# From the last FFN step to the mixer's first weights: residual inside the FFN's accumulation, LayerNorm scale and shift applied as columns, beta and decay from unsplit tokens

## The chip, the core and the metric

The program runs on one NeuronCore of a Trainium2 chip. The metric is the device time of one execution in microseconds (us), taken as the median of several runs. The core has TensorE (PE, matrix products, with its weight loads shown as PEld), VectorE (DVE), ScalarE (ACT), GpSimd (POOL) and SyncE (SP), which issues the large weight loads. Each engine works through its own instructions in order, and they wait for each other by semaphores.

## What is computed

Two transformer blocks on 256 tokens of width 1024. The first block is attention, then a convolutional feed-forward net (FFN) with residual, then an RMS norm. The second block puts 16 meta tokens in front, applies a LayerNorm, and runs a hybrid mixer (a gated delta rule and a stick-breaking attention), and a mixture of 32 experts. Only the passage between the two blocks is touched:

```python
x = x + _conv_ffn(_rmsnorm(x, norm_ffn[i]), ffn_w_up[i], ffn_conv_w[i], ffn_conv_b[i], ffn_w_down[i])
return _rmsnorm(x, norm_final)
...
h = layer_norm(jnp.concatenate([meta, x], axis=1), ln_emb_g, ln_emb_b)   # ((x - mu) * rsqrt(var + 1e-5)) * g + b
...
proj = x @ w_in
dn_qkv, dn_z, dn_b, dn_a, sb_qkv, gates = jnp.split(proj, SPLIT_POINTS, axis=-1)
beta = jax.nn.sigmoid(dn_b)
g = -jnp.exp(dn_a_log) * jax.nn.softplus(dn_a + dn_dt_bias)
```

The LayerNorm follows an RMS norm, so both are done at once: with y = x * norm_final, the layer norm of y divided by x's root mean square is (y - mean(y)) / sqrt(var(y) + eps), where eps is 1e-5 times (mean(x*x) + 1e-6).

## The kernel before

**Tiles.** X holds the 256 tokens as two tiles t = 0, 1 of 128 tokens by 1024 features. For products the tokens are turned: hT_hi and hT_lo hold 8 blocks k of 128 features by 272 tokens (16 meta, 256 others). A float32 product is made of three float32r products, hi*hi, hi*lo and lo*hi (`split3`, lines 1933 to 1935), so each operand is split: ACT copies to float32r (hi), DVE subtracts (lo).

**Weights** come in granules of 2048 columns. SP loads a granule into one of three buffers `raw` (line 610; the load of granule n waits until granule n - 3 has been split), ACT makes `whi` (`hi_part`, line 827), DVE makes `wlo` (`lo_part`, line 1298). whi and wlo have two buffers each, and a few granules have their own (`OWN_SLOT`). Granules 16 to 48 are the FFN's, granule 49 (`G_IN`) and 50 are the mixer's z gate, 51 and on its q, k and v. Granule 49 shares its buffer with granule 47.

**Last FFN step.** PE adds granule 48's products (`down`) into four banks PM, 12 matmuls a token tile, 24 in all. At the start of the FFN four bf16 matmuls of a zero row clear the banks (line 2093). A semaphore after token tile 0 (`s_ffn`) and one at the end (`s_gran`) let DVE go on.

**Seam** (lines 1451 to 1489 on DVE, 958 to 979 on ACT, 2131 to 2152 on PE). For each token tile DVE adds the banks to X, multiplies by norm_final with a running sum; ACT squares X and the centred product, with sums; ACT takes the root, DVE multiplies by the LayerNorm's scale row and, in two halves, by the reciprocal root and adds the shift row. PE turns each half (4 transposes of 128 by 128). ACT and DVE split them. In between PE does 16 small products for the router's constants (36 columns each) and dummy products of 128 by 128 (`keep_warm`, line 1993).

**Beta and decay.** Eight columns of w_in (`wba`) are split too, and `ba` is 24 matmuls (8 blocks, three products). The result is turned by `baT`, and DVE and ACT make beta and the decay from it in steps on 12 columns (`decays`, lines 1582 to 1584, and `softplus`, lines 1588 to 1601).

**Order.** After the seam a list `plan` sets the order for all engines. It begins: ba; granule 49's first half; baT; decays; its second half; softplus; granule 50; masks; granule 51. On DVE, `lo_part` of granule 51 stands at "granule 50", so behind softplus.

Of the kernel before, what the change touches and what calls it, by code (L numbers as in the profile page):

```python
# [87 lines left out]
def build(nc, a, out):  # L88
    with ExitStack() as ctx:
# [14 lines left out]
        def con(name, n=None, rows=P):  # L104
# [15 lines left out]
        OWN_SLOT = (14, 15, 48)  # L120
# [9 lines left out]
        scratch = place("scratch", [P, TT, D], PH + 49152)  # L130
        scratch2 = place("scratch2", [P, TT, D], PH + 57344)
# [3 lines left out]
               for n, at in zip(OWN_SLOT, (PH + 74752, PH + 24576, PH + 24576))}  # L135
# [6 lines left out]
        zero = place("zero", [1, D], PH + 96256, BF16)  # L142
# [15 lines left out]
        zsum, nmu, vs, ve = tiny(TT), tiny(TT), tiny(TT), tiny(TT)  # L158
        mx, nmx, psum_, rinv = tiny(8), tiny(8), tiny(8), tiny(8)
# [16 lines left out]
        s_zero, s_x2 = sem("s_zero"), sem("s_x2")  # L176
# [10 lines left out]
        assert OWN_SLOT == (G_WO + 2, G_WO + 3, G_IN - 1)  # L187
# [302 lines left out]
        E_STEPS = {"baT": 1, "norm": 2, "D": 1, "orms": 1, "Zs": 3}  # L490
# [47 lines left out]
        wr_experts = place("wr_experts", [P, GROUPS, KD, EPG], PH + 65536)[:, :, :, :]  # L538
        wr_groups = place("wr_groups", [P, KD, GROUPS], PH + 65536 + 4 * NE * KD)[:, :, :]
# [154 lines left out]
        def _(pool):  # L694
# [19 lines left out]
            pool.dma_start(vrow[112:113, 1, :], a["dn_norm_g_2"]).then_inc(s_vrow, 16)  # L714

            pool.wait_ge(s_cols, 1)
# [26 lines left out]
            pool.memset(ba, 0.0).then_inc(s_init, 1)  # L743
            pool.memset(sbk[:, :, NT:3 * P], 0.0).then_inc(s_init, 1)
# [73 lines left out]
        def _(act):  # L818
# [91 lines left out]
            act.wait_ge(s_colsT, 1)  # L910
            act.activation(cols[:, 0:P + 113], PM[:, 1, 0:P + 113], ACT.Copy).then_inc(s_cols, 1)
# [12 lines left out]
            act.wait_ge(s_cols, 1)  # L924
# [10 lines left out]
            def ffn_step(n, j, par, it, first=False, last=False):  # L935
# [8 lines left out]
                if not last:  # L944
                    hi_part(n + 3, it)
                act.wait_ge(s_hid, j + 1)
                act.activation(hid_hi[:, par, :, :], hid[:, par, :, :], ACT.Copy).then_inc(s_hidhi, 1)
                if not first:
                    hi_part(n + 4, it)
# [8 lines left out]
            act.wait_ge(s_wba, 48)  # L958
# [328 lines left out]
        def _(dve):  # L1287
# [165 lines left out]
            for t in range(TT):  # L1453

                if t == 0:
                    dve.wait_ge(s_ffn, 1)
                else:
                    dve.wait_ge(s_gran, G_IN)
# [1188 lines left out]
```

## Time and profile before

| | us |
|---|---|
| median of 3 runs | 858.91 |
| lowest, highest | 858.44, 859.41 |
| the profiled execution | 859.89 |
| its span, first to last instruction | 857.8 |

The span is the part that the trace shows; some 2 us of the execution lie around it. The profile has a page with the busy time of each engine, a chain of the work that ended last, and views of stretches: instructions in order of time, and busy time with the granted clock. PE's matmuls are pipelined: a row's duration reaches from its start to a modelled end, and the distance between starts is what a matmul costs in a row of them. A plain float32 matmul shows as two records.

### The profile page before, as it was taken

The page shows a single profiled execution, that of the slowest core. Times are in us where ns is not written, and L with a number is a line of the kernel's source. Part 1 is how long each engine was busy: PE and PEld are TensorE (multiplying, and loading weights), DVE is VectorE, ACT ScalarE, POOL GpSimd, SP SyncE. Part 2 cuts the span into 40 slices and gives each one's busy share as a digit, 9 for nine tenths or more (in the row PEclk, how much of TensorE's full clock was granted, in tenths as well). Part 3 has the DMA queues.
Part 4 walks back from the last instruction along what each step waited for, and adds up shares of the span by engine and source line. Part 5 has one row for each costly group of instructions (what it writes and reads, how often), then busy time and mean ns, then how long its engine had stood idle before and what let it go on. Part 6 is the DMA issues. An engine that isn't in the chain of part 4 may idle for free.

```text
span 857.8 us, 16132 instructions
## 1 busy us (share of the span) xinstructions
PE 831.0 (97%) x6642; PEld 681.0 (79%) x6642; DVE 483.9 (56%) x829; ACT 374.0 (44%) x559; POOL 57.7 (7%) x91
## 2 busy tenths in 40 slices
PE   6999999999999999999999999999999999999994
PEld 6999999999999988998898999999755555555541
DVE  4455667776667777666733445486753333333335
ACT  4555764455545554566453454654321111111113
POOL 0200041000000000100110000000110000000010
PEclk9999999999999998999999999999999999999998
DMA  9864362555555561444333232559889999999981
GB/s 289 272 218 136 128 194 83 182 192 193 173 180 187 196 196 56 142 129 146 119 99 99 90 110 66 181 196 412 341 335 408 409 409 409 408 409 409 409 352 50
DMA packets 102129, 193.29 MB, mean 225 GB/s; under 512 B 4589, under 2 KB 70464, under 8 KB 101936
## 3 DMA queue, kind: packets, MB, share of 16 engines
q1 hardware_dynamic: 99664, 185.61, 60.3%
q0 software_dynamic: 1824, 4.60, 1.7%
q10 hardware_dynamic: 576, 2.14, 0.7%
q8 instruction: 49, 0.80, 0.4%
q14 instruction: 16, 0.13, 0.0%
HBM read 191.29 MB, written 1.05 MB: 224 GB/s over the span
## 4 chain that ended last, share of the span: by engine, by line
PE 87%; DVE 6%; ACT 3%; issue 2%; DMA 1%; ACTq 0%; DVEq 0%
PE PG L1933 14%; PE PG L2503 13%; PE PG L1935 13%; PE PG L1934 13%; PE PG L2525 7%; PE PM L2534 4%; PE PM L1933 2%; PE PM L1935 2%; PE PM L1934 2%; ACT whi L827 2%; PE PG L2512 1%; PE PM L2357 1%; DVE wlo L1298 1%; PE PG L1993 1%; PE PM L2475 1%
## 5 line engine op out<-in xcount | busy, mean ns | idle before, releaser
L1933 PE MATMUL PG<-hT_hi,whi 128*128 128x256 f32 (+1 forms) x832 | 240.1, 289 | 0.0
L1935 PE MATMUL PG<-hT_hi,wlo 128*128 128x256 f32 (+1 forms) x832 | 235.0, 282 | 0.0
L1934 PE MATMUL PG<-hT_lo,whi 128*128 128x256 f32 (+1 forms) x832 | 234.9, 282 | 0.0
L1298 DVE TENSOR_TENSOR wlo<-raw,whi 128x2048 fp32r<-128x2048 f32 x75 | 171.8, 2290 | 76.5 <-ACT whi L827 76.3
L1933 PEld LDWEIGHTS PG<-hT_hi,whi 128*128 128x128 f32 x832 | 156.9, 189 | 5.9 <-issue 2.6
L1935 PEld LDWEIGHTS PG<-hT_hi,wlo 128*128 128x128 f32 x832 | 157.1, 189 | 0.0
L1934 PEld LDWEIGHTS PG<-hT_lo,whi 128*128 128x128 f32 x832 | 156.5, 188 | 0.2
L827 ACT ACTIVATE whi<-raw 128x2048 fp32r<-128x2048 f32 x75 | 143.2, 1910 | 25.5 <-PE PG L1935 22.6
L2503 PE MATMUL PG<-expert_w,xw 128*64 128x256 f32 x992 | 113.9, 382 | 0.0
L1860 DVE SCALAR_TENSOR_TENSOR y_lo<-PG,small,y_hi 128x512 fp32r<-128x512 f32 x32 | 24.0, 750 | 133.2 <-ACT y_hi L1229 133.2
L2503 PEld LDWEIGHTS PG<-expert_w,xw 128*64 128x64 f32 x992 | 68.6, 137 | 37.0 <-issue 5.8
L2525 PE MATMUL PG<-expert_w,hid 128*64 128x512 f32 x256 | 61.9, 604 | 0.0
L1229 ACT ACTIVATE y_hi<-PG,small 128x512 fp32r<-128x512 f32 x32 | 22.0, 688 | 85.6 <-PE PG L2525 85.6
L1223 ACT ACTIVATE gusum<-PG 128x256 f32<-128x256 f32 x32 | 12.3, 385 | 97.2 <-PE PG L2503 97.2
L2525 PEld LDWEIGHTS PG<-expert_w,hid 128*64 128x64 f32 x256 | 15.6, 136 | 29.7 <-issue 29.6
L1933 PE MATMUL PG<-whi,hT_hi 128*128 128x256 f32 x128 | 36.8, 288 | 1.3 <-DVE hT_lo L1560 0.9
L1935 PE MATMUL PG<-whi,hT_lo 128*128 128x256 f32 x128 | 36.0, 281 | 0.0
L1934 PE MATMUL PG<-wlo,hT_hi 128*128 128x256 f32 x128 | 35.9, 281 | 0.0
L786 POOL COPY xw<-pair 128x512 f32 x31 | 19.6, 634 | 200.5 <-PE PG L2503 182.2
L1933 PE MATMUL PM<-whi,hid_hi 128*128 128x512 f32 x80 | 31.6, 395 | 0.2 <-DVE wlo L1298 0.2
L1935 PE MATMUL PM<-whi,hid_lo 128*128 128x512 f32 x80 | 31.2, 390 | 0.0
L1934 PE MATMUL PM<-wlo,hid_hi 128*128 128x512 f32 x80 | 31.2, 390 | 0.0
(496 smaller groups left out, 1289.8 us busy)
## 6 DMA issues: line engine op xcount, KB each, us to landing
expert_w<-in_expert_w_gate SPq DMA_DIRECT2D x64, 512.0 KB, 15.4
expert_w<-in_expert_w_up SPq DMA_DIRECT2D x64, 512.0 KB, 15.8
expert_w<-in_expert_w_down SPq DMA_DIRECT2D x32, 1024.0 KB, 17.0
raw<-in_ffn_w_up SPq DMA_DIRECT2D x22, 1024.0 KB, 5.1
raw<-in_w_in SPq DMA_DIRECT2D x22, 1024.0 KB, 5.2
raw<-in_moba_w_qkv SPq DMA_DIRECT2D x12, 1024.0 KB, 6.0
raw<-in_ffn_w_down SPq DMA_DIRECT2D x11, 1024.0 KB, 4.8
raw<-in_moba_w_o SPq DMA_DIRECT2D x4, 1024.0 KB, 5.1
```

The source lines that it names most:

```text
L786: pool.tensor_copy(xw[i2][:, :, :], pair[:, :, bass.ds(at, WIN)]).then_inc(s_win, 1)
L827: act.activation(hi_of(n), raw[:, n % R, :], ACT.Copy).then_inc(s_hi, 1)
L1223: act.activation(gusum[i2][:, :], PG[:, i2, 0:EFF], ACT.Copy).then_inc(s_gu, 1)
L1229: act.activation(y_hi[:, :], result, ACT.Copy, scale=slotw[i2]).then_inc(s_yhi, 1)
L1298: dve.tensor_tensor(lo_of(n), raw[:, n % R, :], hi_of(n).bitcast(F32), ALU.subtract).then_inc(s_lo, 1)
L1860: dve.scalar_tensor_tensor(y_lo[:, :], result, slotw[i2], y_hi[:, :].bitcast(F32), ALU.mult, ALU.subtract).then_inc(s_y, 1)
L1933: pe.matmul(dst, lh, rh, start=start, stop=False, **kw)
L1934: pe.matmul(dst, lh, rl, start=False, stop=False, **kw)
L1935: return pe.matmul(dst, ll, rh, start=False, stop=stop, **kw)
L2503: mm = pe.matmul(PG[WIN * h:WIN * h + WIN, i2, 0:EFF], x[:, KH * kind + k, :], w[:, h, k, :], start=kind + k == 0, stop=kind == 1 and k == ...
L2525: mm = pe.matmul(result[WIN * h:WIN * h + WIN, :], hid2[i2][:, f, :], w[:, f, 512 * h:512 * h + 512], start=f == 0, stop=f == 1)
L2534: mm = pe.matmul(PM[:, 2 * t + h, :], hot[i2][x, P * t:P * t + P], y[x, :], start=first and y is y_hi, stop=last and y is y_lo)
```

## The change

1. The zero matmuls go. The four banks are begun with X itself, by float32 matmuls of the identity (`start_sums`, 128 by 512). Three stand where 10 of 12 dummy products were, the last where the zero matmuls were. After the FFN the banks hold X plus its sum.
2. Granule 49 gets an own buffer. On ACT its hi part moves ahead of `hid_hi`.
3. DVE multiplies the banks by norm_final straight away. Token tile 0's mean and variance come from bn_stats and bn_aggr, tile 1's from a running sum on DVE and a square on ACT. X gets only (y - mean) / root, by `tensor_scalar` halves.
4. PE turns these. Scale and shift are applied on the turned tokens, per 128-feature block, into `h_cols`: blocks 0 to 3 by DVE, 4 to 7 by ACT, four instructions a token tile each. Two more rows of DMA and one more small transpose bring them as columns (`ln_cols`). The split reads h_cols.
5. `ba` is 8 plain float32 matmuls of h_cols, in two halves of the array (output rows 0 to 7 and 64 to 71), and `baT` 6 small matmuls that add the halves.
6. The rows of X still need scale and shift for the mixer's residual: `shifted_rows`, 8 `tensor_tensor` of 512 columns, each waiting for the one before, between `lo_part` of granule 50 and the plan.
7. Router products and dummy products on PE are put in another order. Three memsets on POOL wait for granule 49.

```diff
+            start_sums(0, 0)
+            start_sums(0, 1)
+            start_sums(1, 0)
+            keep_warm(2, con("ident"), con("ident"), PM[:, 3, :])
             norm_T(1, 1)
             pe.wait_ge(s_ev, evacs(G_FFN - 1))
-            for b in range(4):
-                pe.matmul(PM[:, b, :], zero[0:1, 0:P], zero[0:1, 0:512], start=True, stop=True)
+            start_sums(1, 1)
...
+            def columns(t):
+                act.wait_ge(s_xT, 11 + 2 * t)
+                for k in range(KH, KD):
+                    act.activation(h_cols[:, k, META + P * t:META + P * t + P], PM[:, 2 * t + 1, P * (k - KH):P * (k - KH) + P], ACT.Identity,
+                                   scale=ln_cols[:, 0, k:k + 1], bias=ln_cols[:, 1, k:k + 1]).then_inc(s_hcolsa, 1)
...
+            def columns_hi(t, f):
+                act.wait_ge(*((s_hcolsv, KH * t + KH) if f == 0 else (s_hcolsa, 1 + KH * t + KH)))
+                c = slice(META + P * t, META + P * t + P)
+                ln_hi(hT_hi[:, 4 * f:4 * f + 4, c], h_cols[:, 4 * f:4 * f + 4, c])
...
+            def shifted_rows(t):
+
+                for f in range(2):
+                    c = slice(D // 2 * f, D // 2 * f + D // 2)
+                    step(dve.tensor_tensor(X[:, t, c], X[:, t, c], rows[:, 3, c], ALU.mult))
+                    step(dve.tensor_tensor(X[:, t, c], X[:, t, c], rows[:, 0, c], ALU.add))
...
             lo_part(G_IN + 1)
+            shifted_rows(0)
+            shifted_rows(1)
             for st in plan:
...
+                    for k in range(0, KD, 2):
+                        if k == KH:
+                            pe.wait_ge(s_hcolsa, 1 + KD)
+                        for h in range(2):
+                            mm = pe.matmul(bank[WIN * h:WIN * h + 8, 0:NT], wba[:, k + h, :], h_cols[:, k + h, :], start=k == 0, stop=k == KD - 2)
```

**DVE, from the seam's last splits to the decays.** The hT_lo rows are the last splits of the turned tokens, wlo is granule 50, the rows on `small` are `decays`. Before:

```order
L1481 TENSOR_TENSOR hT_lo<-PM,hT_hi 128x4x128 [waits s_xhi] x4
L1298 TENSOR_TENSOR wlo<-raw,whi 128x2048 [waits s_hi]
L1582 TENSOR_TENSOR small<-small 128x12 [waits s_wba,pm_free1]
L1583 TENSOR_SCALAR small<-small 128x12 [waits s_dve]
L1584 TENSOR_TENSOR small<-small 128x12 [waits s_dve]
```

Now:

```order
L1527 TENSOR_TENSOR hT_lo<-h_cols,hT_hi 128x4x128 [waits s_xhi] x4
L1326 TENSOR_TENSOR wlo<-raw,whi 128x2048 [waits s_hi]
L1534 TENSOR_TENSOR X<-X,rows 128x512
L1535 TENSOR_TENSOR X<-X,rows 128x512 [waits s_dve]
L1534 TENSOR_TENSOR X<-X,rows 128x512 [waits s_dve]
...
L1630 TENSOR_TENSOR small<-small 128x12 [waits s_wba,pm_free1,s_dve]
```

Eight row operations now stand between granule 50's split and the decays.

**PE, from the router's products to `ba`.** `PG<-small` and `PG<-bwr` are the router's products, `PG<-cst` 128x128 dummy products, `PM<-cst,X` the transposes. Before:

```order
L2138 MATMUL PG<-small,cst 128x36 x7
L2140 MATMUL PG<-bwr,cst 128x36 x8
L2142 MATMUL PG<-small,cst 128x36 [waits s_wr]
L1993 MATMUL PG<-cst 128x128 x2
L2148 MATMUL PM<-cst,X 128x128 [waits s_h]
L2148 MATMUL PM<-cst,X 128x128 x3
...
L1993 MATMUL PG<-cst 128x128 x6
```

Now, from tile 0's second half (the rows left out are three more such groups, and the first transposes of tile 1 end the piece):

```order
L2202 MATMUL PM<-cst,X 128x128 [waits s_h]
L2202 MATMUL PM<-cst,X 128x128 x3
L2195 MATMUL PG<-small,cst 128x36
L2196 MATMUL PG<-bwr,cst 128x36
L2041 MATMUL PG<-cst 128x128
...
L2210 MATMUL PG<-small,cst 128x36 [waits s_wr]
L2041 MATMUL PG<-cst 128x128 x3
L2202 MATMUL PM<-cst,X 128x128 [waits s_h]
L2202 MATMUL PM<-cst,X 128x128 x3
```

Half of the router's products moved behind token tile 0's transposes, each pair with a dummy product, and they stand ahead of tile 1's.

**ACT, from tile 1's turned tokens to granule 50.** `mean_wr` is a copy of the router's sums. Before:

```order
L973 ACTIVATE hT_hi<-PM 128x4x128 [waits s_xT] x4
L982 ACTIVATE mean_wr<-PG 128x36 [waits s_logit]
L982 ACTIVATE mean_wr<-PG 128x36
L827 ACTIVATE whi<-raw 128x2048 [waits s_gran,landed2]
L1002 ACTIVATE baT<-PM 8x272 [waits pm_full0]
```

Now:

```order
L999 ACTIVATE h_cols<-PM,small 128x128 [waits s_xT]
L999 ACTIVATE h_cols<-PM,small 128x128 x3
L983 ACTIVATE hT_hi<-h_cols 128x4x128 [waits s_hcolsv]
L983 ACTIVATE hT_hi<-h_cols 128x4x128 [waits s_hcolsa]
L1015 ACTIVATE mean_wr<-PG 128x36 [waits s_logit]
L1015 ACTIVATE mean_wr<-PG 128x36
L830 ACTIVATE whi<-raw 128x2048 [waits s_gran,landed2]
```

Four column operations came in ahead of tile 1's two copies, and so ahead of granule 50's hi part.

## Rows read from the trace of the kernel before

**Rows 1.** The page: busy us of each engine (share of the span), instructions.

```profile
PE 831.0 (97%) x6642; PEld 681.0 (79%) x6642; DVE 483.9 (56%) x829; ACT 374.0 (44%) x559; POOL 57.7 (7%) x91
```

**Rows 2.** Chain that ended last, over the seam: start, us, what.

```profile
318.06 1.93 ACT whi L827
320.01 1.36 DVE wlo L1298
...
336.19 1.79 PE PG L1993 x16
```

**Rows 3.** PE in order of time: start, us, engine, line, what.

```profile
323.95 0.67 PE L2133 MATMUL PG<-cst,MT 16*128 16x16 f32 x8
324.55 1.98 PE L2138 MATMUL PG<-small,cst 128*128 128x36 f32 x16
...
328.25 0.41 PE L2142 MATMUL PG<-small,cst 1*128 1x36 f32 x2
...
330.18 1.97 PE L2148 MATMUL PM<-cst,X 128*128 128x128 f32 x8 [0.72 <-DVE X L1476]
...
340.80 0.28 PE L1933 MATMUL PG<-hT_hi,whi 128*128 128x256 f32 x1
```

**Rows 4.** PE where granule 51 begins.

```profile
352.59 0.35 PE L1933 MATMUL PG<-hT_hi,whi 128*128 128x272 f32 x1
```

**Rows 5.** DVE in order of time, 316 to 355 us.

```profile
316.11 0.69 DVE L1430 TENSOR_TENSOR hid<-cgate,cup 128x512 f32<-128x512 f32 x1
...
323.61 1.23 DVE L1463 CUSTOM_DVE_ANT_0 XN<-X,rows 128x1024 f32<-128x1024 f32 x1
...
344.58 0.17 DVE L1582 TENSOR_TENSOR small<-small 128x12 f32<-128x12 f32 x1 [3.44 <-ACT small L1002]
...
346.30 0.17 DVE L1588 TENSOR_SCALAR small<-small 128x12 f32<-128x12 f32 x1 [1.14 <-ACT small L1090]
...
350.14 2.29 DVE L1298 TENSOR_TENSOR wlo<-raw,whi 128x2048 fp32r<-128x2048 f32 x1
352.35 0.68 DVE L1606 TENSOR_TENSOR dN<-cst,small 128x512 f32<-128x512 f32 x1
```

**Rows 6.** ACT in order of time, 312 to 346 us.

```profile
312.52 1.02 ACT L932 ACTIVATE cup<-PG,cols 128x256 f32<-128x256 f32 x2 [0.53 <-PE PG L1935]
316.84 0.63 ACT L947 ACTIVATE hid_hi<-hid 128x512 fp32r<-128x512 f32 x1 [3.29 <-DVE hid L1430]
...
336.72 0.29 ACT L982 ACTIVATE mean_wr<-PG 128x36 f32<-128x36 f32 x2
336.88 1.93 ACT L827 ACTIVATE whi<-raw 128x2048 fp32r<-128x2048 f32 x1
...
345.86 0.21 ACT L1088 ACTIVATE small<-small 128x12 f32<-128x12 f32 x1
```

**Rows 7.** Stretches: us, PE, PEld, DVE, ACT, POOL busy, PEclk, DMA, GB/s.

```profile
328.00:330.00 2.00, 1.46 (x9) 1.08 (x8) 1.65 (x3) 1.07 (x3) 0.00 (x0) 0.75 0.00 0
330.00:332.00 2.00, 1.82 (x9) 1.82 (x10) 2.00 (x4) 0.98 (x3) 0.00 (x0) 0.50 0.00 0
...
334.00:336.00 2.00, 2.00 (x12) 2.00 (x11) 1.09 (x2) 0.40 (x1) 0.00 (x0) 0.55 0.03 8
...
403.00:405.00 2.00, 0.59 (x5) 0.42 (x4) 1.99 (x3) 0.38 (x1) 0.00 (x0) 1.00 0.00 0
```

**Rows 8.** PE elsewhere: the FFN's start, and two forms in the expert stage.

```profile
128.38 1.03 PE L1927 MATMUL PG<-cst,XN 128*128 128x128 f32 x8
...
133.87 1.32 PE L1927 MATMUL PG<-cst,XN 128*128 128x128 f32 x8 [0.34 <-DVE XN L1384]
135.13 1.03 PE L2093 MATMUL PM<-zero 1*128 1x512 bf16 x4
...
824.87 3.67 PE L2503 MATMUL PG<-expert_w,xw 128*64 128x256 f32 x32
...
831.74 1.02 PE L2545 MATMUL PM<-X,alpha_ident 128*128 128x512 f32 x2
```

More of the change, by code:

```diff
@@ L129, in build @@
         oT_lo = place("oT_lo", [P, KD, SEQ], PH + 57344, F32R)
-        scratch = place("scratch", [P, TT, D], PH + 49152)
-        scratch2 = place("scratch2", [P, TT, D], PH + 57344)
+        squares_of = [place(f"squares{i}", [P, D], PH + 71680 + 4096 * i) for i in range(3)]
         prob = place("prob", [P, 2, 2, 3 * P], PH + 98304)
@@ L923, in _ @@
             norm_hi(1, [1])
-            act.wait_ge(s_cols, 1)
+            act.wait_ge(s_cols, 2)
             def col(i, n=1):
@@ L945, in ffn_step @@
                     hi_part(n + 3, it)
+                else:
+                    hi_part(n + 4, it)
                 act.wait_ge(s_hid, j + 1)
                 act.activation(hid_hi[:, par, :, :], hid[:, par, :, :], ACT.Copy).then_inc(s_hidhi, 1)
-                if not first:
+                if not first and not last:
                     hi_part(n + 4, it)
@@ new lines, in _, with ln_hi @@
+            squares(0)
+            act.wait_ge(s_ve, 1)
+            act.activation(lnrt[:, 0:1], lnmv[:, 1:2], ACT.Sqrt, bias=ve[:, 0:1]).then_inc(s_lnrt, 1)
+            def ln_hi(dst, src):
+                act.activation(dst, src, ACT.Copy).then_inc(s_xhi, 1)
+            act.wait_ge(s_xT, 9)
+            act.activation(h_cols[:, :, 0:META], PG[:, 0, 0:P].rearrange("p (k n) -> p k n", k=KD), ACT.Copy).then_inc(s_hcolsa, 1)
+            act.wait_ge(s_hcolsa, 1)
+            ln_hi(hT_hi[:, :, 0:META], h_cols[:, :, 0:META])
@@ L1465, in _, with two @@
-            for t in range(TT):
+            dve.wait_ge(s_rows, 64)
+            dve.wait_ge(s_ffn, 1)
+            def two(x):
+                return x.rearrange("p (h n) -> p h n", h=2)
+            dve.tensor_tensor(two(XN[:, 0, :]), PM[:, 0:2, :], two(rows[:, 2, :]), ALU.mult).then_inc(s_x2, 1)
+            dve.wait_ge(s_x2, 1)
+            for b in range(2):
+                step(dve.bn_stats(lnst[:, 6 * b:6 * b + 6], XN[:, 0, D // 2 * b:D // 2 * b + D // 2]))
+            step(dve.bn_aggr(lnmv[:, 0:2], lnst[:, 0:12]))
@@ L2262, in _ @@
                     for c, (t0, n) in enumerate(CH):
-                        mm = pe.transpose(bank[0:n, 8 * c:8 * c + 8], baT[:, t0:t0 + n], con("ident", 8, 8))
+                        for h in range(2):
+                            mm = pe.matmul(bank[0:n, 8 * c:8 * c + 8], baT[:, h, t0:t0 + n], con("ident", 8, 8), start=h == 0, stop=h == 1)
                     mm.then_inc(full(*st), 1)
```

188 lines of the change are left out of this document (100 added, 88 removed).

## The prediction

> **What bounds the kernel now.** The page comes first: PE is busy 97% of the span, DVE 56%, ACT 44% [rows 1]. So time is won or lost where PE waits or does filler. The chain of waits gives such a place. For 18 us, from 318.06 to 336, it runs through ACT's and DVE's split of granule 49 and DVE's and ACT's norm, and it ends in PE's transposes and dummy products [rows 2]. PE in order of time tells the same: it leaves the FFN at 323.95, does router products and fillers, waits 0.72 us for DVE's first half, and takes up weights of the mixer, granule 49, at 340.80 [rows 3]. That is 16.9 us in which it does little that counts.
>
> The second place to read is the one behind it, where a gain must pass. Granule 51 begins on PE at 352.59 [rows 4]. On DVE its split runs from 350.14, and the next instruction starts at 352.35 [rows 5]. So PE is served 0.2 us ahead of need. Ahead of that split DVE does the decays and softplus, and before the decays it idles 3.44 us [rows 5].
>
> Last the clock. The granted clock falls from 2.4 to 1.2 GHz at 329.0 (0.75 on average over 328 to 330), after the stretch of 36-column products, and is back at 2.4 GHz only at about 335.8 (0.55 over 334 to 336); an idle time of 1.4 us near 404 left it at 2.4 GHz [rows 7].
>
> **FFN start: +0.1 us.** Three 512-column sums replace ten dummies. One such matmul in the expert stage shows as 1.02 us with its end [rows 8], 0.87 from start to start, so three and two dummies of 0.22 are 3.05 us from 130.8. PE is then at 133.85, where it anyway waits until 133.87 for DVE [rows 8]. The fourth costs 0.9 to 1.0 against 0.96 for the zero matmuls it replaces (135.13 to 136.09) [rows 8]. The extra small transpose on PE lies on the path, 0.1 us. Its two DMAs, one ACT copy, and POOL's later queue (0.25 us) are hidden: ACT and POOL idle there for longer.
>
> **Seam on DVE and ACT.** Granule 49's hi part now runs on ACT from 313.5 to 315.5, in the 3.29 us in which ACT waits for `hid` [rows 6]; nothing but hid_hi is queued behind it. DVE splits it right behind hid_lo, 318.2 to 320.4, and starts the norm when PE has ended token tile 0, the twelfth of the 24 matmuls that end at 323.95, at 321.4 instead of 322.4. DVE then does a product (1.25 us by the row of 1024 columns [rows 5]), two statistics of 512 columns (0.65 each, an estimate from the 0.69 of a 512-column operation [rows 5]), three small ones and tile 1's product, 1.25. Its first half of X is there at 326.5, the second at 327.0. PE comes for it at 323.95 + 0.6 for the meta transposes + 2.7 for half the router products = 327.3 and does not wait. Of those products 16 take 324.55 to 328.25, 0.23 each [rows 3], and each pair has a dummy of 0.22. So the wait of 0.72 us is gone, and PE sets the pace next.
>
> **Seam on PE.** From 327.3: two half tiles of four transposes at 0.11 each, 0.9 (eight took 1.03 with the end at 2.4 GHz [rows 8]), 328.2; the other router products 2.7, 330.9; the bias product 0.3 and three dummies 0.7, 331.9; tile 1's transposes 0.9, 332.8. DVE's halves of tile 1 would be there at 330.5, since ACT's two squares and root end by 329.2. Eight dummies bring PE to 334.5. Then `ba`. Sixteen float32 matmuls of 256 columns in two halves of the array took 3.67 us [rows 8], so eight of 272 columns are 1.95 us: 336.45. If the halves did not run side by side it would be 3.9. It needs h_cols at 334.3 (below) and granule 49 needs the last split at 336.2; both are met. **PE takes up granule 49 at 336.45 instead of 340.80, 4.35 us sooner** [rows 3].
>
> **Where that goes.** PE then does 11.8 us of work until granule 51 (340.80 to 352.59 in rows 3 and 4), plus 0.3 for the three more baT matmuls, and arrives at 348.55. What it waits for there:
> - tile 1's turned tokens, 332.85;
> - ACT's four column operations. No row has 128 columns with scale and bias; two of 256 take 1.02 us [rows 6], 0.46 from start to start, and 128 columns fewer save 0.1: 0.36 each, 1.45 together, 334.3. The ends are 0.2 (a plain small copy) and 0.46, so 0.8 to 1.9;
> - two hT_hi copies of 512 columns at 0.55, 335.4; mean_wr 0.16 (336.72 to 336.88), granule 50's hi part 1.93 [rows 6], 337.5;
> - DVE's split of it, 2.25 as for granule 51 [rows 5], 339.75;
> - the eight row operations. Each is like the 512-column product of 0.69 [rows 5] plus 0.03 for its wait: 5.75, 345.5. What hid nothing before is now in front of the decays: these stand behind it in DVE's queue, and ACT's exponentials and softplus behind them;
> - three decays 0.6, 346.1. Before, ACT's next step waited for a table load until 345.86 [rows 6]; now the table is long there;
> - ACT 0.44 (345.86 to 346.30), softplus 3.84 (346.30 to 350.14), the split 2.25 [rows 5, 6]: 352.65.
>
> **So granule 51 starts at 352.7, where it started at 352.59.** The gain of 4.35 us ends in a wait of PE of 4.15 us, and 0.1 is lost. Bounds: the column operations 0.8 to 1.9, the row operations 0.66 to 0.75 each; together -1.0 to +0.8.
>
> Here a page gives another price. The Trainium skill, "VectorE: DVE Perf Modes", section on the TRN2 errata, has 172 + columns cycles at 1.2 GHz for a ScalarE operation from PSUM, 0.25 us for 128 columns; by it the columns take 1.0, not 1.45, and the sum comes 0.45 lower. The same section warns of many small tiles for this fixed part, which speaks against eight column operations where there was none. The 256-column row shows more than that formula, so I keep to the row.
>
> **The clock behind the wait: +1.7 us.** The trace has no idle time of PE of 4 us in its middle. One of 1.4 us left the clock up [rows 7]; a stretch of thin work of some 5 us took it down. 4.15 us with nothing is more than either, so I take it that the clock falls. In the one case shown it stayed at 1.2 GHz for 5.5 us after PE took up work again (330.18 to 335.8) [rows 3, 7]; all work behind 352.7 is dense, so each microsecond there at 1.2 GHz costs half. That is 0 to 2.75; I take 1.7, above the middle, because the row's 5.5 held idle time and thin work and this stretch does not last so long, but a fall is likelier than none. The Trainium skill, "TensorE: Matmul & The Clock Gate", Part 1, says that the slow state is the default and activity lifts it; by that the fall is certain, and the sum would hold.
>
> Does anything take this up later? The split of granule 52 and the masks on DVE follow that of 51 directly and end at 358.0, before PE wants granule 52 even by the old time of 360.9. Behind that the kernel is PE's, and the experts' loads wait for PE's progress. So it passes through. POOL's three memsets now run at 342.5, 18 us before POOL's next task.
>
> **Sum:** 0.1 + 0.1 + 1.7 = +1.9 us. The profiled execution took 859.89 with a span of 857.8; that is 1 us above the median of 858.91. On the median: **860.8 us**.
>
> **Rivals.**
> *The clock also falls in the seam.* It did before, and the router products are as thin as before. Against it: the dummies between them, and no idle time. If it falls at 329, the work of PE from there (2.0 router, 0.3, 0.7, 0.9) takes up to 3.6 us more, and all that hangs on 332.85 moves by as much: +3.6 + 1.9 = 864.4. Decides: the clock over 329 to 333. 0.23.
> *The wait without the cost.* PE waits some 4 us, the clock stays up, and 858.3 to 859.9 comes out, nearest 859.1. It needs a clock that rides over an idle time three times that of the row. 0.17.
> *The row operations are cheap* (the rival on the other side). If an operation of 512 columns in SBUF cost 0.42 instead of 0.72, eight would give back 2.4 us, PE would wait 1.8, too short for the clock to fall: granule 51 at 350.3, 856.7. It decides from about 0.5 each. The 0.69 row speaks against it. With it I count anything unseen that shortens DVE's chain. 0.10.
> *My forecast*, 859.6 to 861.9: 0.50.
>
> **Numbers.** 0.2%, 1.7 us, is about what a measurement can tell from no change: 857.2 to 860.6. Of the forecast's 0.50 some 0.18 falls under 860.6; of the first rival all is slower; the second is no change. Slower 0.55, same 0.35, faster 0.10. The range has to take in most of the clock rival and the lower end of the cheap wait: 858.2 to 864.0.
>
> **What the new profile would show.** PE takes up granule 49 near 336.5 and waits about 4 us before granule 51 for the split on DVE; the eight row operations stand from 339.8 to 345.5 with 0.69 each; the granted clock is 1.00 from 324 to 350 and lower behind 351. I am wrong if PE's first matmul of granule 51 comes without a wait, if the clock falls before 333, or if `ba` takes near 4 us.

## The result, and the profile after

The changed kernel takes 860.93 us (median of 7 runs, 860.43 to 862.50), where the kernel before took 858.85 beside it (857.92 to 859.41). The ratio is 1.0029, with a 95% interval of 1.0020 to 1.0039: slower by 2 us. The profiled execution took 860.89 with a span of 859.0, against 859.89 and 857.8 before. Two kernels below have one slow execution each, of 1027 and of 4567 us: the ratios leave these out, the medians 857.66 and 862.24 don't, and without them they would be 857.54 and 861.75. Lines of `kernel.py` below are those of the changed kernel unless a section says otherwise.

The page first, which answers to [rows 1]:

```profile
PE 829.3 (97%) x6634; PEld 677.8 (79%) x6634; DVE 487.1 (57%) x840; ACT 375.4 (44%) x567; POOL 58.2 (7%) x93
```

PE is busy 1.7 us less than before and the span is 1.2 us longer. So PE waits more, 2.9 us in all. The view of PE in order of time shows where (start, us, engine, line, what, and in brackets the idle time before it and what ended it):

```profile
323.99 0.67 PE L2188 MATMUL PG<-cst,MT 16*128 16x16 f32 x8
...
327.38 1.04 PE L2202 MATMUL PM<-cst,X 128*128 128x128 f32 x8
...
332.13 1.04 PE L2202 MATMUL PM<-cst,X 128*128 128x128 f32 x8
333.00 1.95 PE L2041 MATMUL PG<-cst 128*128 128x128 f32 x16
334.88 2.01 PE L2324 MATMUL PM<-h_cols,small 128*8 128x272 f32 x16
336.82 0.38 PE L1981 MATMUL PG<-hT_hi,own_hi 128*128 128x256 f32 x1
...
339.85 1.24 PE L2332 MATMUL PM<-cst,baT 8*128 8x8 f32 x12
```

```profile
353.20 0.56 PE L1981 MATMUL PG<-hT_hi,whi 128*128 128x272 f32 x1 [3.43 <-DVE wlo L1326]
```

Granule 49 is taken up at 336.82, where it was 340.80 [rows 3]: 4.0 us won. Granule 51 begins at 353.20, where it was 352.59 [rows 4]: the 4.0 us are gone, and 0.6 more, in a wait of 3.43 us for DVE's split. DVE in order of time shows what stands ahead of that split, and answers to [rows 5]:

```profile
321.45 1.23 DVE L1484 TENSOR_TENSOR XN<-PM,rows 128x1024 f32<-128x1024 f32 x1 [0.98 <-PE PM L1983]
...
337.76 2.29 DVE L1326 TENSOR_TENSOR wlo<-raw,whi 128x2048 fp32r<-128x2048 f32 x1 [1.21 <-ACT whi L830]
339.97 0.68 DVE L1534 TENSOR_TENSOR X<-X,rows 128x512 f32<-128x512 f32 x1
340.69 0.69 DVE L1535 TENSOR_TENSOR X<-X,rows 128x512 f32<-128x512 f32 x1
...
345.77 0.17 DVE L1630 TENSOR_TENSOR small<-small 128x12 f32<-128x12 f32 x1
...
346.92 0.17 DVE L1636 TENSOR_SCALAR small<-small 128x12 f32<-128x12 f32 x1 [0.56 <-ACT small L1118]
...
350.76 2.29 DVE L1326 TENSOR_TENSOR wlo<-raw,whi 128x2048 fp32r<-128x2048 f32 x1
352.97 0.68 DVE L1654 TENSOR_TENSOR dN<-cst,small 128x512 f32<-128x512 f32 x1
```

From 339.97 to 345.77 DVE does the eight row operations (two of them are shown). Before, the decays began at 344.58, after an idle time of 3.44 us [rows 5]; now they begin at 345.77 behind work. ACT in order of time answers to [rows 6]:

```profile
313.51 1.92 ACT L830 ACTIVATE own_hi<-raw 128x2048 fp32r<-128x2048 f32 x1
...
333.21 1.50 ACT L999 ACTIVATE h_cols<-PM,small 128x128 f32<-128x128 f32 x4 [0.88 <-PE PM L2202]
334.59 1.16 ACT L983 ACTIVATE hT_hi<-h_cols 128x512 fp32r<-128x512 f32 x2
...
346.48 0.21 ACT L1116 ACTIVATE small<-small 128x12 f32<-128x12 f32 x1 [3.61 <-DVE small L1632]
```

Last the clock. Stretches with busy time by engine and, behind POOL, PE's granted clock, as in [rows 7]:

```profile
328.00:330.00 2.00, 2.00 (x21) 2.00 (x19) 1.43 (x5) 0.39 (x2) 0.00 (x0) 1.00 0.00 0
...
350.00:352.00 2.00, 0.00 (x0) 0.00 (x0) 1.86 (x5) 2.00 (x2) 0.00 (x0) 1.00 0.00 0
352.00:354.00 2.00, 0.80 (x3) 0.83 (x4) 2.00 (x3) 0.26 (x1) 0.00 (x0) 0.70 0.00 0
354.00:356.00 2.00, 2.00 (x10) 2.00 (x10) 2.00 (x5) 0.00 (x0) 0.00 (x0) 0.50 0.91 252
356.00:358.00 2.00, 2.00 (x17) 2.00 (x16) 2.00 (x2) 0.00 (x0) 0.00 (x0) 0.95 0.78 272
```

The seam is now at 2.4 GHz throughout. Behind the wait the clock is 1.2 GHz until about 356.2. PE has dense work from 353.20, so some 3 us of it ran at 1.2 GHz, with 10 matmuls in 2 us where 18 are usual. What that cost shows at the first product of a later stage, now and in the profile before:

```profile
360.67 1.95 PE L2349 MATMUL PM<-cst,dN 128*128 128x128 f32 x16
```

```profile
358.71 1.95 PE L2280 MATMUL PM<-cst,dN 128*128 128x128 f32 x16
```

From granule 51's start it is 7.47 us away, and was 6.12: 1.35 us lost. With the 0.61 by which granule 51 starts later that makes 1.96. The span grew by 1.2 only: the profile before has one more fall of the clock, near 610 us (mean 0.86 over 608 to 620, where this profile has 1.00), and its way from 566.74 to its end is 0.8 us longer than the same way here. That place is far behind the change, and five of the twelve profiles in this document have such a fall, whatever the kernel.

### The profile page after: what moved, and what is told of

Its sections match the earlier page's. It is cut to its first block, busy times and chain, and to the rows that moved or that the text cites. A ratio compares the mean times of both kernels' runs of the same rounds, so it can differ in the third digit from the quotient of the medians.

```text
span 859.0 us, 16131 instructions
## 1 busy us (share of the span) xinstructions
PE 829.3 (97%) x6634; PEld 677.8 (79%) x6634; DVE 487.1 (57%) x840; ACT 375.4 (44%) x567; POOL 58.2 (7%) x93
## 4 chain that ended last, share of the span: by engine, by line
PE 85%; DVE 8%; ACT 4%; issue 2%; DMA 1%; ACTq 0%; DVEq 0%
PE PG L1981 13%; PE PG L2572 13%; PE PG L1983 12%; PE PG L1982 12%; PE PG L2594 7%; PE PM L2603 4%; PE PM L1981 2%; PE PM L1982 2%; PE PM L1983 2%; ACT whi L830 2%; DVE wlo L1326 2%; PE PG L2581 1%; PE PM L2426 1%; PE PG L2041 1%; PE PM L2057 1%
## 5 line engine op out<-in xcount | busy, mean ns | idle before, releaser
L1981 PE MATMUL PG<-hT_hi,whi 128*128 128x256 f32 (+1 forms) x816 | 236.2, 289 | 3.4 <-DVE wlo L1326 3.4
L1983 PE MATMUL PG<-hT_hi,wlo 128*128 128x256 f32 (+1 forms) x816 | 231.1, 283 | 0.0
L1982 PE MATMUL PG<-hT_lo,whi 128*128 128x256 f32 (+1 forms) x816 | 231.0, 283 | 0.0
L1326 DVE TENSOR_TENSOR wlo<-raw,whi 128x2048 fp32r<-128x2048 f32 x74 | 169.5, 2291 | 74.6 <-ACT whi L830 74.5
L1981 PEld LDWEIGHTS PG<-hT_hi,whi 128*128 128x128 f32 x816 | 154.6, 189 | 9.7 <-issue 6.5
L1983 PEld LDWEIGHTS PG<-hT_hi,wlo 128*128 128x128 f32 x816 | 154.7, 190 | 0.0
L1982 PEld LDWEIGHTS PG<-hT_lo,whi 128*128 128x128 f32 x816 | 154.2, 189 | 0.2
L830 ACT ACTIVATE whi<-raw 128x2048 fp32r<-128x2048 f32 x74 | 141.3, 1909 | 24.9 <-PE PG L1983 22.5
```

The costliest lines, as they stand in the source:

```text
L830: act.activation(hi_of(n), raw[:, n % R, :], ACT.Copy).then_inc(s_hi, 1)
L1326: dve.tensor_tensor(lo_of(n), raw[:, n % R, :], hi_of(n).bitcast(F32), ALU.subtract).then_inc(s_lo, 1)
L1981: pe.matmul(dst, lh, rh, start=start, stop=False, **kw)
L1982: pe.matmul(dst, lh, rl, start=False, stop=False, **kw)
L1983: return pe.matmul(dst, ll, rh, start=False, stop=stop, **kw)
```

## The experiments

The theory: DVE's chain (tile 1's turned tokens, columns, copies, split, eight row operations, decays, softplus, split) sets the start of granule 51, so what PE wins at granule 49 becomes a wait, and the wait takes the clock down. The rivals: another link sets granule 51; the clock's fall costs nothing; the fall comes from the seam. Where a ratio is given, it is against runs of the kernel before on the same chip. The profiles differ by up to 0.5 us already where PE leaves the FFN, and no view shows why; a table behind the last run counts from there.

### The row operations later

```diff
             lo_part(G_IN + 1)
-            shifted_rows(0)
-            shifted_rows(1)
...
                         lo_part(n + 1)
+                    if n in (G_IN + 2, G_IN + 3):
+                        shifted_rows(n - G_IN - 2)
```

> The changed kernel with one edit: the eight row operations on X stand on VectorE behind the splits of granules 52 and 53 (four behind each), no longer ahead of the decays. My theory, that the gain at granule 49 is lost again in VectorE's chain ahead of granule 51 and that the clock falls in PE's wait there: the chain ends 5.8 us sooner than it must, so PE takes up granule 51 without a wait at about 349.8 (changed kernel: 353.20 after 3.43 of waiting), the granted clock is 1.00 over 350 to 356, and the time is 3.4 + 1.45 = 4.9 us below the changed kernel: 856.0, 0.997 of the kernel before. Rival A, the wait is real but the clock's fall costs nothing: 857.5. Rival B, what holds granule 51 is not the row operations but another link (exponentials, table load, the raw buffer of granule 51): granule 51 stays near 353 and the time at 860.9. Rival C, the row operations only move the wait to granules 52 to 54, where VectorE has splits and masks to do: 351 is early but a wait of 2 us or more shows behind it, and the time is 858 to 860.

Measured: 856.31 us, ratio 0.9967 (0.9955 to 0.9980). PE at granule 51, then a stretch:

```profile
349.69 0.36 PE L1981 MATMUL PG<-hT_hi,whi 128*128 128x272 f32 x1
```

```profile
352.00:354.00 2.00, 2.00 (x18) 2.00 (x17) 2.00 (x3) 0.08 (x1) 0.00 (x0) 1.00 0.97 345
```

No wait, 3.5 us sooner (0.2 of it by an earlier end of the FFN), and the clock stays up. The row operations were the link. They don't pass the wait on to granules 52 to 54: from granule 51 to the later stage PE takes 6.12 us, as in the kernel before. Rivals A, B and C fall: 4.6 us of the 4.9 expected are there by the medians, 5.3 by the ratios.

### Filler inside the wait

```diff
                         pe.wait_ge(s_ev, evacs(n - 2))
+                        if n == G_IN + 2:
+                            keep_warm(14, con("ident"), con("ident"))
```

> The changed kernel with one edit: PE does 14 dummy products of 128 by 128 (about 3.0 us of dense work at 2.4 GHz) just ahead of granule 51, inside the wait for its split. Nothing else moves, and VectorE's chain ends at the same time, so granule 51 still begins at 353.2 to 353.3. Theory (the fall of the clock in the wait costs 1.45 us): the granted clock is 1.00 over 352 to 358, and the time is 1.4 to 1.5 us below the changed kernel, 859.4 to 859.5, 1.0007 of the kernel before. Rival A (the clock's fall costs nothing, or falls anyway): same as the changed kernel, 860.9 (1.0024). Rival D (dummies come out too long and stand in the way of granule 51): 861 or more, with granule 51 later than 353.5.

Measured: 859.06 us, ratio 1.0006 (0.9996 to 1.0016). PE around granule 51, and the stretch behind it:

```profile
349.24 3.29 PE L2041 MATMUL PG<-cst 128*128 128x128 f32 x28
352.75 0.39 PE L1981 MATMUL PG<-hT_hi,whi 128*128 128x272 f32 x1 [0.22 <-DVE wlo L1326]
```

```profile
354.00:356.00 2.00, 2.00 (x19) 2.00 (x18) 2.00 (x5) 0.00 (x0) 0.00 (x0) 1.00 0.98 329
```

Here PE still can't begin before DVE is done, and it does nothing useful in the meantime; the time falls by 1.9 us all the same, and the rival by which the fall of the clock costs nothing is out. Granule 51 stands 0.45 sooner than in the first profile, but 0.37 of that is an earlier end of the FFN. From granule 51 to the later stage PE takes 6.15 us, 1.3 less than the 7.47 of the first profile and 2.7 less than the 8.88 of the repeat below; the 1.9 of the medians lies between. In three of 11 executions the mean granted clock was 0.994 and the time 860.2 to 860.5, in the others 0.995 or 0.996; where it fell in those three no trace shows. A fall near 610 would explain some 0.7 of the 1.1 to 1.4 us that they took more.

### Half the row operations

```diff
             shifted_rows(0)
-            shifted_rows(1)
```

> The changed kernel with one edit: the four row operations of token tile 1 are left out, so that the residual of tile 1 in the mixer lacks LayerNorm's scale and shift; this is a probe of time. It doses the suspected cost. Theory: VectorE's chain is 4 x 0.73 = 2.9 us shorter, granule 51 begins at 350.3 with a wait of about 0.5 us, too short for the clock to fall, and the time is 2.9 + 1.45 = 4.35 us below the changed kernel: 856.6 (0.9974 of the kernel before). Rival A (no cost of the clock): 858.0 (0.999). Rival B (the row operations don't set granule 51): 860.9 (1.0024).

Measured: 857.22 us, ratio 0.9976 (0.9967 to 0.9985). PE at granule 51:

```profile
350.62 0.36 PE L1980 MATMUL PG<-hT_hi,whi 128*128 128x272 f32 x1 [1.03 <-DVE wlo L1326]
```

This kernel leaves the second token tile's residual without scale and shift, so it is a probe of time only. Half the dose moves the start by 2.4 us from the FFN's end (2.6 as the rows stand) where 2.9 was expected, and the clock stayed at 2.4 GHz behind a wait of 1.03 us. The time is 3.7 us below the changed kernel by the medians, where 4.35 was expected. The missing 0.5 at granule 51 stands in one operation of softplus, a `tensor_scalar` of 12 columns, which took 0.68 instead of 0.18. Its cause comes further down.

### Without the dummies between the router's products

```diff
                     pe.matmul(PG[:, 1, 64:64 + NL], con("ones"), bwr[:, k, :], start=False, stop=False, skip_group_check=True)
-                    keep_warm(1, con("ident"), con("ident"))
```

> The changed kernel with one edit: the eight dummy products between the pairs of router products go, so that the 36-column products stand side by side as in the kernel before. It tests the rival of the prediction by which thin products take the clock down in the seam. If they do, the granted clock is below 1.00 somewhere in 328 to 336, tile 1's turned tokens are complete 1 to 2.5 us later than without a fall, and the time is at or above the changed kernel: 861 to 864. If the clock stays up, PE has 8 x 0.22 = 1.8 us less to do, reaches token tile 0 sooner (where it may wait up to 0.5 us for VectorE's first half), turns tile 1 about 1.2 us sooner, VectorE's chain ends about 1.2 us sooner, and the time is 1.2 us below the changed kernel: 859.7 (1.001). I give the fall 0.6, since the kernel before fell behind the same products.

Measured: 859.75 us, ratio 1.0003 (0.9993 to 1.0014), with executions from 857.96 (mean granted clock 0.995) to 861.67 (0.990). The median alone would fit the branch without a fall. The profiled execution, of 861.45 us, shows the other one; stretches, then PE at granule 51:

```profile
326.00:328.00 2.00, 1.97 (x11) 1.94 (x11) 1.45 (x6) 1.44 (x4) 0.00 (x0) 0.55 0.00 0
...
334.00:336.00 2.00, 2.00 (x11) 2.00 (x11) 1.75 (x5) 0.90 (x3) 0.00 (x0) 0.50 0.00 0
```

```profile
355.23 0.36 PE L1981 MATMUL PG<-hT_hi,whi 128*128 128x272 f32 x1 [2.85 <-DVE wlo L1326]
```

The clock was at 1.2 GHz from 326 to 336, and granule 51 came 2.0 us later than in the changed kernel (2.6 from the FFN's end). Yet this wait, of 2.85 us, left the clock up, so the sum is +0.6 against 860.89. The fall in the seam is thus real in this execution. The mean clocks, from 0.990 to 0.995, say that its size differs from one execution to the next, and at 0.995 it may be missing; no trace shows those.

One thing the median does say: this kernel is 1.2 us faster than the changed kernel, by the ratios 2.2, and the intervals of the two ratios don't meet. The eight dummies are 1.8 us of PE's way through the seam, and here they cost more than they saved. One reason is in the profile: with the seam longer, the wait behind it left the clock up. How long the seam was in the faster executions no trace shows; the profiled one is the second longest of ten.

### The kernel before, with dummies between the same products

```diff
                 pe.matmul(PG[:, 1, 0:NL], con("ones"), wr[:, k, :], start=k == 0, stop=k == KD - 1)
+                keep_warm(k % 2, con("ident"), con("ident"))
             for k in range(KD):
                 pe.matmul(PG[:, 1, 64:64 + NL], con("ones"), bwr[:, k, :], start=k == 0, stop=False)
+                keep_warm(k % 2, con("ident"), con("ident"))
...
-            keep_warm(2, con("ident"), con("ident"))
```

> The kernel before with one edit: a dummy product of 128 by 128 behind each second of the 16 router products in the seam, eight more, and the two behind the bias product gone. It asks how much of the changed kernel's gain at granule 49 (4.35 us) was the clock: the kernel before spent 329 to 335.8 at 1.2 GHz. If the dummies keep the clock up, PE comes to tile 0 at 330.4, turns it in 1.0 instead of 2.0 us, does six dummies in 1.3 instead of 2.8, turns tile 1 when VectorE has it (333.0 to 334.1), is through its eight dummies at 335.9 and takes up granule 49 at 338.9 to 339.0 instead of 340.80; VectorE's and ScalarE's steps behind the seam all follow PE's, so granule 51 comes 1.85 us sooner, and the time is 1.85 below the kernel before: 857.1 (0.998). Rival A: the clock falls all the same, at the wait for tile 0's half, and the time is 858.9 to 859.7 (1.000 to 1.001), since eight dummies are added. Rival B: the clock stays up and granule 49 comes sooner, but the decays, which wait for a table load and ba, hold granule 51 at 352.6: 858.9.

Measured: 857.66 us, ratio 0.9985 (0.9976 to 0.9994). PE in order of time (lines of the kernel before), then a stretch:

```profile
330.13 1.09 PE L2149 MATMUL PM<-cst,X 128*128 128x128 f32 x8
...
332.80 1.32 PE L2149 MATMUL PM<-cst,X 128*128 128x128 f32 x8 [0.23 <-DVE X L1476]
...
339.02 0.28 PE L1933 MATMUL PG<-hT_hi,whi 128*128 128x256 f32 x1
...
350.79 0.36 PE L1933 MATMUL PG<-hT_hi,whi 128*128 128x272 f32 x1
```

```profile
330.00:332.00 2.00, 2.00 (x19) 1.95 (x19) 1.93 (x5) 1.34 (x4) 0.00 (x0) 1.00 0.03 8
```

Granule 49 comes at 339.02 instead of 340.80, and granule 51 at 350.79 instead of 352.59. PE left the FFN 0.3 sooner here (323.64 against 323.95), so 1.5 of the 4.0 us that the change won at granule 49 can be had by the dummies alone. In this kernel they pass through, because DVE's decays follow PE and not a queue of their own: 1.5 at granule 51, and 1.3 in the time, where 1.85 was expected.

### The own buffer alone

```diff
-        OWN_SLOT = (14, 15, 48)
+        OWN_SLOT = (14, 15, 48, 49)
...
             pool.memset(ba, 0.0).then_inc(s_init, 1)
+            pool.wait_ge(s_gran, G_IN + 1)
...
+                else:
+                    hi_part(n + 4, it)
                 act.wait_ge(s_hid, j + 1)
...
-                if not first:
+                if not first and not last:
                     hi_part(n + 4, it)
```

> The kernel before with one part of the change alone: granule 49 gets an own buffer, and on ScalarE its hi part stands ahead of hid_hi; scratch tiles move to make room for it. VectorE then splits granule 49 at about 318 and can start the norm when PE ends token tile 0, at 321.4 instead of 322.4. By the prediction's step that is 1.0 us on all that follows, up to granule 51, so long as nothing else holds it: PE comes for tile 0's first half at 329.5, which would then be there, so 0.7 us of PE's wait goes and the rest of the norm comes 1.0 us sooner: 857.9 (0.9988). If the clock then stays up for longer, since the idle time is gone, up to 1.8 us more: 856.1. If the norm is set by ScalarE's squares and not by VectorE's start, nothing is won: 858.9.

Measured: 858.81 us, ratio 1.0001 (0.9992 to 1.0010). The expectation of 1.0 us failed. (The scratch tiles and two router tables are placed elsewhere to make room; the diff leaves that out.) DVE and POOL in order of time, and PE at granule 51 (its own lines):

```profile
320.96 1.22 DVE L1462 TENSOR_TENSOR X<-X,PM 128x1024 f32<-128x1024 f32 x1 [0.79 <-PE PM L1938]
...
344.65 1.37 DVE L1595 TENSOR_SCALAR small<-small 128x12 f32<-128x12 f32 x1
```

```profile
344.59 0.47 POOL L745 MEMSET sbk<- 128x448 f32 x1 [9.24 <-PE PG L1938]
345.00 0.53 POOL L746 MEMSET sbv<- 128x512 f32 x1
345.46 0.53 POOL L747 MEMSET dU<- 128x512 f32 x1
```

```profile
351.24 0.36 PE L1936 MATMUL PG<-hT_hi,whi 128*128 128x272 f32 x1 [1.03 <-DVE wlo L1301]
```

DVE begins the norm sooner, as meant. But an operation on 12 columns, 0.17 elsewhere [rows 5 has others of this size], takes 1.37 and ends at 346.02, as the third memset does (345.46 + 0.53 = 345.99). The memsets have come there because the new buffer shares memory with what the first two of them clear, so they wait for granule 49. PE pays 1.03 us for it. (This profile is of a short execution, 857.81 us, in which the clock fell for less of the seam, 0.86 on average over 324 to 336 against 0.72 before. Granule 51 stands 1.35 us sooner in it than before, 0.4 of it by an earlier end of the FFN, although the median has not moved.)

### The own buffer, with the memsets one granule later

```diff
-            pool.wait_ge(s_gran, G_IN + 1)
+            pool.wait_ge(s_gran, G_IN + 2)
```

> The kernel before with granule 49's own buffer, as in the run with that alone, and GpSimd's three memsets waiting for granule 50 instead of 49. In that run VectorE's tensor_scalar of softplus took 1.37 us beside the memsets (344.65 to 346.02; the third memset ended at 345.99), and PE waited 1.03 us ahead of granule 51, so that the slot's gain of 1.0 us at the norm's start was gone. Theory: the operation takes 0.17, the split ends 1.2 us sooner, the wait goes, and the time is 1.0 us lower: 857.8, 0.9988 to 0.999 of the kernel before. Rival: the gain is covered by where the clock falls in the seam: 858.8, 1.000.

Measured: 857.23 us, ratio 0.9986 (0.9977 to 0.9995). The same operation:

```profile
346.08 0.18 DVE L1595 TENSOR_SCALAR small<-small 128x12 f32<-128x12 f32 x1
```

PE begins granule 51 without a wait. The profiled execution was one with a long fall of the clock in the seam (0.72 over 324 to 336; 858.56 us), so its times are no good for a comparison with the run above; the two ratios are. They differ by 0.0015, 1.3 us, where 1.0 was expected, though the intervals still overlap. The profile before has the same 0.72 in the seam: against it, granule 49 and granule 51 both come 0.6 us sooner, counted from the FFN's end.

### Another order of the seam, and the best version

```diff
             turned_half(0, 1)
-            router_sums(4, KD)
-            pe.wait_ge(s_wr, 176)
-            pe.matmul(PG[:, 1, 64:64 + NL], con("ones", rows=1), rb[0:1, :], start=False, stop=True, skip_group_check=True).then_inc(s_logit, 1)
-            keep_warm(3, con("ident"), con("ident"))
+            router_sums(4, 6)
+            keep_warm(4, con("ident"), con("ident"))
             turned_half(1, 0)
             turned_half(1, 1)
-            keep_warm(8, con("ident"), con("ident"))
+            router_sums(6, KD)
+            pe.wait_ge(s_wr, 176)
+            pe.matmul(PG[:, 1, 64:64 + NL], con("ones", rows=1), rb[0:1, :], start=False, stop=True, skip_group_check=True).then_inc(s_logit, 1)
+            keep_warm(1, con("ident"), con("ident"))
```

> The kernel with the late row operations, and PE's seam in another order: between token tile 0's and tile 1's transposes stand two pairs of router products instead of four, then four dummy products; the last two pairs and the bias product stand behind tile 1's transposes, where eight dummies stood and are gone. PE has as much filler as work there, so the clock should stay at 2.4 GHz. Theory (VectorE's chain from tile 1's turned tokens sets granule 51, with PE close behind): tile 1 is turned at about 331.5 instead of 332.8, the columns, copies and splits behind it come 1.3 us sooner, ba can begin at 333.4 and granule 49 near 335.3, granule 51 near 348.4, and the time is 1.3 us below the late kernel: 855.0, 0.9953 of the kernel before. Rival 1: the clock falls among the router products (four thin pairs behind each other near the end), up to 3 us lost: 856 to 859. Rival 2: VectorE's halves of tile 1 are not there before 331.0, so that only 0.5 us is won: 855.8.

Measured: 855.76 us, ratio 0.9962 (0.9949 to 0.9975), where the late kernel had 856.31 and 0.9967. That is at most half of the 1.3 us expected, and within the noise. In the traces granule 49 comes 0.9 sooner from the FFN's end, granule 51 only 0.5. DVE, POOL and PE:

```profile
342.92 0.91 DVE L1640 TENSOR_SCALAR small<-small 128x12 f32<-128x12 f32 x1
```

```profile
343.27 0.53 POOL L748 MEMSET sbv<- 128x512 f32 x1
```

```profile
349.04 0.36 PE L1981 MATMUL PG<-hT_hi,whi 128*128 128x272 f32 x1 [0.57 <-DVE wlo L1326]
```

The same cause again: the operation ends at 343.83, the memset at 343.80, and PE waits 0.57 us. The last version moves the memsets behind granule 50:

```diff
-            pool.wait_ge(s_gran, G_IN + 1)
+            pool.wait_ge(s_gran, G_IN + 2)
```

> The kernel with the late row operations and the new order of the seam, and one edit more: GpSimd's three memsets wait for granule 50, no longer for granule 49. In the trace of that kernel VectorE's second tensor_scalar of softplus, 12 columns, took 0.91 us where it takes 0.17 in the kernel before, and it ended at 343.83, as the second memset did (343.27 + 0.53); PE then waited 0.57 us ahead of granule 51. Theory: the memset holds that operation up. With the memsets behind granule 50 (near 349, beside a split or the masks, which are tensor_tensor) it takes 0.17, the split of granule 51 ends 0.74 sooner, PE doesn't wait, and the time is 0.57 us lower: 855.2 (0.9955 of the kernel before). Rival: the 0.91 has another cause (its own operands): then it stays, and so does 855.8. Rival on the other side: the memsets now hold up the masks or the split of granule 52: 856 or more.

Measured: 855.01 us, ratio 0.9960 (0.9947 to 0.9974). DVE and PE:

```profile
342.79 0.17 DVE L1640 TENSOR_SCALAR small<-small 128x12 f32<-128x12 f32 x1
```

```profile
348.18 0.36 PE L1981 MATMUL PG<-hT_hi,whi 128*128 128x272 f32 x1
```

In the trace the operation takes 0.17, PE's wait is gone and granule 51 begins at 348.18, 4.4 us sooner than in the kernel before. From the FFN's end to granule 51 it is 0.74 less than in the run above, which is what the operation had lost. The median is 0.75 lower too, but the two intervals overlap almost wholly, so of this last step only the trace speaks. Against the kernel before this version is 3.7 us faster; against the changed kernel 5.9 by the medians.

### The changed kernel again

> The changed kernel again, as the base of the comparisons on one chip. 860.9 (1.0029 of the kernel before), and a profile with a wait of 3.4 us ahead of granule 51. The executions of the changed kernel seen so far had a mean granted clock of 0.990 to 0.994: a second profile tells whether the clock's fall stands at the same place each time. By my theory it is always behind the wait; if the seam's thin products also take it down in some executions, it stands at 326 to 336 in those.

Measured: 862.24 us, ratio 1.0036 (1.0023 to 1.0049). Stretches behind the wait:

```profile
352.00:354.00 2.00, 0.83 (x4) 0.86 (x5) 2.00 (x3) 0.23 (x1) 0.00 (x0) 0.63 0.00 0
354.00:356.00 2.00, 2.00 (x10) 2.00 (x10) 2.00 (x5) 0.00 (x0) 0.00 (x0) 0.50 0.85 228
356.00:358.00 2.00, 2.00 (x10) 2.00 (x10) 2.00 (x2) 0.00 (x0) 0.00 (x0) 0.50 0.84 296
358.00:360.00 2.00, 2.00 (x13) 2.00 (x12) 0.36 (x1) 0.00 (x0) 0.00 (x0) 0.66 0.19 36
```

Granule 51 begins at 353.17 behind 3.44 us of waiting, all as in the first profile, but 1.2 GHz lasts until 359.4 instead of 356.2, for 6.2 us of PE's work instead of 3.0. The later stage is 8.88 us behind granule 51's start, so 2.76 us are lost against 1.35 in the first profile. One place and one wait have two prices. They are not the whole difference of the two executions, 863.04 and 860.89: the other 0.7 lies at the second place, near 610, where this profile falls and the first doesn't:

```profile
612.00:614.00 2.00, 2.00 (x5) 1.65 (x6) 1.97 (x4) 0.00 (x0) 0.00 (x0) 0.50 1.03 410
```

Five of the twelve profiles have this second fall (0.86 to 0.90 over 608 to 620, or 0.86 over 596 to 608), and from a wait near 565 to the end they take 290.8 to 291.1 us, the other seven 290.2 to 290.5. So an execution's mean clock alone doesn't tell which price it paid behind the wait.

The table counts all profiles from where PE leaves the FFN (its first small transposes), in us. The last column is from granule 51's start to the first product of the later stage.

| kernel | PE leaves the FFN | to granule 49 | to granule 51 | from 51 to the later stage |
|---|---|---|---|---|
| before | 323.95 | 16.85 | 28.64 | 6.12 |
| changed | 323.99 | 12.83 | 29.21 | 7.47 |
| changed, again | 323.96 | 12.82 | 29.21 | 8.88 |
| row operations later | 323.81 | 12.82 | 25.88 | 6.12 |
| filler in the wait | 323.62 | 12.83 | 29.13 | 6.15 |
| half the row operations | 323.82 | 12.82 | 26.80 | 6.13 |
| without the dummies | 323.45 | 15.98 | 31.78 | 6.12 |
| before, with dummies | 323.64 | 15.38 | 27.15 | 6.12 |
| own buffer | 323.57 | 14.69 | 27.67 | 6.13 |
| own buffer, memsets later | 323.45 | 16.25 | 28.04 | 6.11 |
| other order | 323.66 | 11.89 | 25.38 | 6.13 |
| best | 323.54 | 11.88 | 24.64 | 6.13 |

## Why the prediction was right

The prediction was 860.8 us (858.2 to 864.0), slower by the likeliest case. It was right, and by the mechanism it gave; that the number lies so near is partly luck, as the sum below shows. Point by point:

- **FFN start, +0.1.** The first product of the FFN stands at 136.20 against 136.09. Right.
- **DVE's norm 1.0 us sooner.** It starts at 321.45, PE comes for the first half at 327.38 and doesn't wait. Right. What it is worth by itself shows only once the memsets are out of the way: that own-buffer kernel is 1.2 us faster than the kernel before by the ratio, and 0.6 of it stands between the FFN's end and granule 51.
- **The seam keeps its clock.** The mean granted clock over 324 to 336 was 1.00 in all eight profiles of kernels with a dummy between the router's products, and 0.59 to 0.86 in all four without (the kernel before 0.72). The rival that had 0.23 is out, and the argument against it, the dummies, is shown. (Its price was added up wrongly: 2.0, 0.3, 0.7 and 0.9 at half speed take 3.9 us more, not 3.6.)
- **Granule 49, 4.35 us sooner.** It was 3.98: PE began `ba` at 334.88 and not 334.5. `ba` took 1.94 for 1.95.
- **PE's work up to granule 51.** Mis-sized. Three more `baT` matmuls were put at 0.3; the piece took 1.17 us from 339.85 to the next product, where the three before took 0.24. The 0.9 us cost nothing, since PE had to wait anyway: 3.43 instead of 4.15.
- **DVE's chain, 352.7.** It was 353.20. The column operations took 1.38 from the first to the copies (1.45 forecast), the eight row operations 5.80 (5.75), softplus 3.84 (3.84). The 0.5 comes from the start, where ACT begins tile 1's columns at 333.21 and not 332.85, and from the 0.23 us between DVE's next operation and PE's first product (0.24 in [rows 4, 5]), which the sum left out.
- **The clock, +1.7 with bounds 0 and 2.75.** 1.35 in the first profile and 2.76 in the second; the filler run puts it at 1.9 on the median. The value was near, and the upper bound was met by luck: 1.2 GHz lasted 6.2 us in the second, longer than the 5.5 from [rows 3, 7], but each microsecond of it cost 0.44 and not half (10 matmuls in 2 us instead of 18).
- **The sum, +1.9.** It was +2.1 by the medians, and 1.96 in the first profile: +0.61 at granule 51, where +0.2 was expected with the FFN's 0.1, and 1.35 of the clock, where 1.7 was. The two misses nearly cancel, which is luck. So is the median: an execution with the long fall pays 1.4 us more.
- **POOL's memsets** were held for free. In the changed kernel they are: they run at 344.16 to 345.55, beside row operations that took 0.69 as everywhere. In five other kernels they held up a `tensor_scalar` by 0.15 to 1.2 us. The prediction asked when POOL is needed next, and not what runs on DVE at that time.

Of the price for columns, the trace has 0.35 us each from start to start (1.38 for four). By the formula in the Trainium skill, "VectorE: DVE Perf Modes", section on the TRN2 errata, it would be 0.25; the measurement decides, and the row of 256 columns had been the better guide.

What stays open: what decides between the short and the long fall of the clock, why it falls near 610 in some executions, and where it fell in the three slower executions of the filler run.

## What to carry to other kernels

A gain ahead of a hand-over is worth no more than the slower queue behind it lets through: add up the other engine's chain to the next hand-over, and put work that nobody waits for behind the last split that somebody does. Moving eight operations by two granules turned a loss of 2 us into a gain of 2.8. Where PE must wait, dense dummies inside the wait cost nothing and save the clock for the work behind it. Among thin products they take PE's own time: they won 1.3 us in the kernel before, and in the changed kernel, where a wait followed, it was faster without them. Find the wait first, then the dummies.

## What the runs showed of the hardware

- **A wait has a second price, and it varies.** 3.43 us of idle PE took the granted clock from 2.4 to 1.2 GHz for 3.0 us of the dense work behind it in one execution and for 6.2 in another, a loss of 1.35 and 2.76 us; waits of 1.03 and 2.85 us left it up.
- **Thin products let it fall with PE busy throughout.** Without dummies between the 36-column products the clock fell in all four profiles, in one it was at 1.2 GHz from 326 to 336 us with PE busy for 1.97 to 2.00 of every 2 us; with one 128-column dummy behind each pair it stayed up in all eight.
- **GpSimd's memset stops some of VectorE's operations.** A `tensor_scalar` of 12 columns beside memsets of 448 and 512 columns took 0.32, 0.44, 0.68, 0.91 and 1.37 us instead of 0.17, and each time ended 0.02 to 0.03 us after a memset did: after the first in the 0.44 case, the second in the 0.91 case, the third in the others. The one of 0.32 is in the kernel without the dummies:

```profile
347.87 0.32 DVE L1631 TENSOR_SCALAR small<-small 128x12 f32<-128x12 f32 x1
```

`tensor_tensor` of 512 columns took 0.69 beside them as alone. The Trainium skill, "SBUF — State Buffer", section "Who interferes with whom", has this rule: `tensor_scalar` may take a port that it shares with GpSimd, and the loser blocks; `tensor_tensor` with both inputs in SBUF contends with GpSimd's reads only. The traces agree that `tensor_scalar` is blocked and that a memset, which reads nothing, leaves `tensor_tensor` alone; what GpSimd's reads do no run here shows. But the operation that took 1.37 us had started 0.06 us after the first memset and let two later ones go ahead, where those of 0.91 and 0.44, started just as long behind it, let one and none.
